# A two-layer hybrid attention and mixture-of-experts step: modulation pieces placed anew, rotary swap by copies, one branch instead of two, the expert count in a bank of its own

## The reference

```
for l in range(2):
    sh1, sc1, gt1, sh2, sc2, gt2 = split(silu(cond) @ w_ada[l] + b_ada[l])   # 1024 x 6144 per layer
    h = rms_norm(y, g_attn[l]) * (1 + sc1) + sh1
    q, k, v of three kinds = h @ w_in[l]            # neighbourhood, latent (MLA), banded window (SWA)
    mla_q, kpe, swa_q, swa_k get a rotary embedding  # sample tokens only
    y = y + gt1 * (merge of the three attentions @ w_out[l])
    h = rms_norm(y, g_ffn[l]) * (1 + sc2) + sh2
    scores = sigmoid(h @ w_router); each token picks 2 of 16 experts of one group
    y = y + gt2 * sum over its experts of (silu(h @ w_gate) * (h @ w_up) * gate) @ w_down
out = rms_norm(y, g_final)                          # and the new caches of keys and values
```

## Time and profile before

| what | value |
|---|---|
| median of 3 runs (lowest, highest) | 1347.58 us (1346.36, 1349.18) |
| the profiled execution's own time | 1345.4 us |
| its span, first to last instruction | 1343.5 us |
| busy time of PE, DVE, ACT, POOL | 1178.3, 777.1, 623.0, 111.8 us |
| mean granted clock of PE | 0.922 |
| scores and values of layer 0, first score to the output projection | 170.99 to 299.65 us |
| the same of layer 1 | 837.78 to 913.41 us |
| experts' products, last of layer 0, last of layer 1 | end 690.99 and 1299.2 us |

### The profile page before, as it was taken

The page is one execution under the profiler, slowest core; times in us unless marked ns, Lnnn a source line. Parts: engine busy times, 40 slices in busy tenths (PEclk is TensorE's granted clock), DMA queues, the critical chain, the costliest instruction groups (busy, mean ns, idle before and its releaser), DMA issues.

```text
span 1343.5 us, 15058 instructions
## 1 busy us (share of the span) xinstructions
PE 1178.3 (88%) x5638; PEld 858.7 (64%) x5638; DVE 777.1 (58%) x1068; ACT 623.0 (46%) x739; POOL 111.8 (8%) x124
## 2 busy tenths in 40 slices
PE   5599887779879999999948998889769999999956
PEld 4266444345467888888836764555467888888846
DVE  1212343341658888988825023572477898888835
ACT  2100233430346777778622003561237777877721
POOL 4000020000010110111001001100010011101000
PEclk8799999999869999999975999899859999999985
DMA  9973377861738999999829233001218999999612
GB/s 261 337 248 117 103 265 250 254 248 63 297 113 317 368 366 372 376 372 378 311 103 276 79 121 94 15 1 58 74 62 303 372 383 369 376 370 369 243 56 97
DMA packets 88702, 310.23 MB, mean 231 GB/s; under 512 B 31272, under 2 KB 35620, under 8 KB 76348
## 3 DMA queue, kind: packets, MB, share of 16 engines
q1 hardware_dynamic: 65548, 279.17, 57.2%
q0 software_dynamic: 11792, 18.65, 4.6%
q10 hardware_dynamic: 11296, 11.54, 2.7%
HBM read 307.07 MB, written 24.27 MB: 247 GB/s over the span
## 4 chain that ended last, share of the span: by engine, by line
PE 78%; DVE 7%; issue 4%; DMA 4%; ACT 4%; ACTq 2%; SPq 1%; POOL 0%; POOLq 0%; DVEq 0%
PE bank L780 15%; PE bank L1011 13%; PE bank L1005 13%; PE bank L1006 13%; DMA ring<-in_w_ada 3%; ACT work L1206 3%; PE bank L762 3%; PE bank L884 2%; PE bank L995 2%; PE bank L787 2%; PE bank L898 2%; PE bank L985 2%; PE bank L707 1%; ACTq L1178 1%; PE bank L831 1%
## 5 line engine op out<-in xcount | busy, mean ns | idle before, releaser
L1680 DVE TENSOR_TENSOR ring_r<-ring,work_r 128x4096 fp32r<-128x4096 f32 x96 | 421.6, 4417 | 5.8 <-ACT work_r L1256 5.6
L1256 ACT ACTIVATE work_r<-ring 128x4096 fp32r<-128x4096 f32 x96 | 348.5, 3632 | 139.7 <-PE bank L1006 120.7
L1005 PE MATMUL bank<-work_r 128*128 128x512 f32 x768 | 311.9, 406 | 21.5 <-ACT work_r L1256 9.6
L1006 PE MATMUL bank<-work_r 128*128 128x512 f32 x768 | 305.0, 397 | 0.0
L780 PE MATMUL bank<-hT,ring 128*128 128x384 f32 (+1 forms) x640 | 213.2, 492 | 5.2 <-ACT hT L1132 3.8
L1011 PE MATMUL bank<-ring_r,work_r 128*128 128x512 f32 x768 | 195.0, 396 | 0.4 <-DVE ring_r L1680 0.4
L1005 PEld LDWEIGHTS bank<-work_r 128*128 128x128 f32 x768 | 148.4, 193 | 53.6 <-issue 19.2
L780 PEld LDWEIGHTS bank<-hT,ring 128*128 128x128 f32 (+1 forms) x640 | 120.8, 191 | 90.3 <-issue 11.4
L1006 PEld LDWEIGHTS bank<-work_r 128*128 128x128 f32 x768 | 148.0, 193 | 29.7
L1011 PEld LDWEIGHTS bank<-ring_r,work_r 128*128 128x128 f32 x768 | 144.2, 188 | 34.7 <-DVE ring_r L1680 0.8
L1104 ACT ACTIVATE work<-bank 128x384 f32<-128x384 f32 (+6 forms) x79 | 37.4, 495 | 198.7 <-PE bank L780 94.1
(11 more groups left out here) (200 smaller groups left out, 1151.3 us busy)
## 6 DMA issues: line engine op xcount, KB each, us to landing
ring<-in_w_gate SPq DMA_DIRECT2D x32, 2048.0 KB, 7.8
ring<-in_w_up SPq DMA_DIRECT2D x32, 2048.0 KB, 10.8
ring<-in_w_down SPq DMA_DIRECT2D x32, 2048.0 KB, 10.4
ring<-in_w_ada SPq DMA_DIRECT2D x24, 2048.0 KB, 8.6
ring<-in_w_in SPq DMA_DIRECT2D x4, 2048.0 KB, 13.5
work<-yscr ACTq DMA_DIRECT2D x12, 512.0 KB, 6.1
ring<-in_w_out SPq DMA_DIRECT2D x4, 1280.0 KB, 8.3
ring<-in_w_in SPq DMA_DIRECT2D x12, 256.0 KB, 8.5
```

Source lines behind the costliest of these rows:

```text
L1005: mm(b[:], x_hi[:, k, :], hi[:, k, half, :], start=(k == 0), stop=False)
L1006: last = mm(b[:], x_lo[:, k, :], hi[:, k, half, :], start=False, stop=False)
L1256: A_(w_hi[:, slot % 2, :], ring[slot][:], ACT.Copy).then_inc(s_hi, 1)
L1680: tt(ring_r[slot][:], ring[slot][:], w_hi[:, slot % 2, :].bitcast(F32), ALU.subtract).then_inc(s_lo, 1)
```

## The change

Six things are changed.

1. Pieces. `ADA_ATT` has 10 pieces instead of 16, one in every second step, with job A before job B. Four pieces of layer 1 (4 to 7) stand between the layers (`BETWEEN`): three A and one B behind the experts, one B behind the first two turned blocks, one B behind the sums, one A behind the spread root and its B between the first two projections. Two pieces (10, 11) stand round the router of layer 1. The router of layer 0 keeps four. The ring order follows, and SP's wait for `s_yl` is moved from the third chunk of layer 1 to its fifth.
2. The SWA swap is done by eight ACT copies per layer between groups of 32 partitions. The four permutation matmuls go, and DVE's nine operations on the three query tiles become three.
3. The count of tokens goes to bank 7, behind the signal that the ranks are done, and DVE reads it after the first expert's tokens are split. The constant `iota` is one higher, so that DVE makes the rank in one operation instead of three.
4. The last list of tokens (`slots(NG - 1)`) is stored behind the first low part of the weights instead of ahead of it.
5. The two branches behind the experts are nested, so that one is passed when no expert has over 128 tokens.
6. The read-back of the experts' rows is three DMAs instead of six.

```diff
-ADA_ATT = [(0, c) for c in range(4, N_ADA)] + [(1, c) for c in range(8)]
-ADA_ROUTE = [(1, c) for c in range(8, N_ADA)]
+ADA_ATT = [(0, c) for c in range(4, 10)] + [(1, c) for c in range(4)]
+ADA_ROUTE = [[(0, 10), (0, 11), (1, 8), (1, 9)], [(1, 10), (1, 11)]]
+ADA_BETWEEN = [(1, c) for c in range(4, 8)]
...
+STREAM[1] = [("ada", *x) for x in ADA_BETWEEN] + STREAM[1] + [("ada", *x) for x in ADA_ROUTE[1]]
...
-    put("iota", i[None, :])
+    put("iota", i[None, :] + 1)
...
+BETWEEN = [f"{kind}{x}{c}" for kind, i in zip("AAABBBAB", (0, 1, 2, 0, 1, 2, 3, 3)) for x, c in [ADA_BETWEEN[i]]]
+BETWEEN_LAST, BETWEEN_ROWS, BETWEEN_SUMS, BETWEEN_SPREAD, BETWEEN_FIRST = (BETWEEN[:4], BETWEEN[4:5], BETWEEN[5:6], BETWEEN[6:7],
+                                                                          BETWEEN[7:])
...
+        def further_passes(eng, most, run, skip, p=1):
+            with eng.If(most > P * p):
+                run(p)
+                if p + 1 < PASSES:
+                    further_passes(eng, most, run, skip, p + 1)
+            with eng.Else():
+                skip(p, PASSES - p)
...
-                    if k == 2:
-                        sp.wait_ge(s_yl[NT - 1], 16 * TOPK * l)
+                    if k == 4:
+                        sp.wait_ge(s_yl[NT - 1], 16 * l)
...
-                read_out(pe, (l, "swk"))
-                b = fill_begin((l, "rk"))
-                filled((l, "rk"), mm(b[:, 0:TS], cv("rot"), swk[:, TP:T], start=True, stop=True))
...
-                read_out(pe, (l, "swq2"))
-                for i in range(3):
-                    b = fill_begin((l, f"rq{i}"))
-                    filled((l, f"rq{i}"), mm(b[:, 0:TS], cv("rot"), swq[:, i, TP:T], start=True, stop=True))
...
+                def swapped_halves(dst, src):
+                    half = HD // 2
+                    for a in range(0, P, half):
+                        to = a ^ half
+                        last = A_(dst[to:to + half], src[a:a + half], ACT.Copy)
+                    return last
+                read_out(act, (l, "swk"))
+                swapped_halves(swk_sw, swk[:, TP:T]).then_inc(s_swapk, 1)
                 for i in range(3):
                     copy((l, f"swq{i}"), swq[:, i, :], T, scale=SCALE)
+                read_out(act, (l, "swq2"))
+                swapped_halves(swq_sw, swq[:, :, TP:T]).then_inc(s_swapq, 1)
...
+                act.wait_ge(s_qkv, l + 1)
                 for i in range(NS + LAG_T):
...
+                    last = mm(b[:, t * NE:(t + 1) * NE], cv("tri"), m[:, t, :], start=(t == 0), stop=True)
+                filled((l, "rank"), last)
                 for t in range(NT):
-                    last = mm(b[:, 3 * NE:4 * NE], ones, m[:, t, :], start=(t == 0), stop=(t == NT - 1))
-                filled((l, "rank"), last)
+                    last = mm(banks[7][:, 0:NE], ones, m[:, t, :], start=(t == 0), stop=(t == NT - 1))
+                last.then_inc(s_counted, 1)
...
+                for j in BETWEEN_LAST if l == 0 else []:
+                    if JOB[1, j][0] == 5:
+                        pe.wait_ge(s_ys, done * NE)
+                    ada(j, 1)
                 pe.wait_ge(s_ys, done * NE)
...
-                    for k in range(TOPK):
-                        act.dma_start(yl[:, t, k, :], yscr[k * T + t * P:k * T + (t + 1) * P, :]).then_inc(s_yl[t], 16)
+                    act.dma_start(yl[:, t], yscr.rearrange("(k t p) d -> t p k d", k=TOPK, p=P)[t]).then_inc(s_yl[t], 16)
+                for j in BETWEEN_LAST + BETWEEN_ROWS if l == 0 else []:
+                    ada_row(1, j)
...
-                chain(nc.vector.tensor_reduce(cnt[:, 0:1], b[:, 3 * NE:4 * NE], AX.X, ALU.max))
-                tc(cnti[:, 0:1], cnt[:, 0:1]).then_inc(s_cnt, 1)
-                evac((l, "rank"), ts(rank, b[:, 0:NT * NE], 1.0, None, ALU.add))
+                evac((l, "rank"), stt(rank, b[:, 0:NT * NE], 1.0, R[4], ALU.add, ALU.mult))
...
-                chain(tt(rank, rank, R[4], ALU.mult))
-                chain(ts(rank, rank, -1.0, None, ALU.add))
...
+                    slots(NG - 1)
                     tokens_rest(0)
+                    if p == 0:
+                        v.wait_ge(s_counted, l + 1)
+                        chain(nc.vector.tensor_reduce(cnt[:, 0:1], banks[7][:, 0:NE], AX.X, ALU.max))
+                        tc(cnti[:, 0:1], cnt[:, 0:1]).then_inc(s_cnt, 1)
+                    v.wait_ge(s_slot, NG * (n + 1))
...
+                for j in BETWEEN_LAST if l == 0 else []:
+                    ada(1, j)
                 add_rows(0)
```

158 lines of the change are left out of this document (88 added, 70 removed).

## The result

The changed kernel takes 1306.85 us (median of 4 runs, 1304.62 to 1314.02) where the kernel before took 1346.97 beside it: ratio 0.9708, 95% interval 0.9686 to 0.973. Run again in a later set it took 1309.60 (1308.92 to 1311.74) against 1347.62, ratio 0.9724 (0.9693 to 0.9754). So 38 to 40 us went, not 29.5. The profiled execution is 1304.66 us, its span 1302.5.

A forecast was written before the change was run, and what follows sets the result against it. PE was taken as the bound, with 78% of the chain. Terms of -19.8 - 5.0 - 1.05 - 0.4 - 3.5 + 1.0 - 0.7 = -29.5 us took 1345.4 to 1315.9, plus 2.2 to the median: 1318 us, range 1309 to 1329.

The forecast's parts named there:

- The 16 pieces explain 53.03 us, 3.31 each: Layer 0's attention: 128.66 us against layer 1's 75.63 without pieces; six pieces fewer at 3.3 gain 19.8 us.
- The second reading: Layer 0's attention: a step with a piece, 6.31 us, less one without, 3.07, prices a piece at 3.24 us.
- The new pattern is the pair that costs 9.38 now: Layer 0's attention: one step with a piece and one without together keep taking 9.38 us.
- Swap: Ahead of the first score: copies replacing swap matmuls gain 2.4 us in layer 0 and 2.6 in layer 1, together 5.0.
- Rank and count in layer 1: Layer 1's routing: DVE loses a 0.62 us wait and most small operations, less one more piece's store; 1.05 us gained.
- Router of layer 0: Rank and count in layer 0: only two of five DVE operations go, as the last piece's jobs remain; 0.4 us gained.
- Last list: Ahead of the experts: DVE's large operation moves before the last list, PE starts 1.75 us earlier per layer; 3.5 gained.
- Between the layers: Layer boundary: queue costs 1.0 us, last A and B 0.5, fewer read-back DMAs gain 0.5; sum 1.0 lost.
- The queue that I feared: Between the layers: first B ahead of turned rows, its store ahead of the first row sum; 1.0 us lost.
- Nested branches: nothing on the path: Behind the experts: engines pass their branches while scatter (3.90 us) or read-back (5.58) runs, so no gain.
- slower than before: Rival on the swap: slow copies between partition groups delay DMA issues in both layers; 1354 us at 6 us each, chance 0.03.
- the warm tail: Rival between the layers: clock stays up through sums of squares, swap and read-back reach their ends; 1311 us, chance 0.08.

The follow-up runs named there:

- e1: Changed kernel with the six moved pieces back (16 in layer 0's attention, two of three steps, B ahead of A, old SP wait): 1332.29 us.
- e9: Changed kernel with the same ten attention pieces in two of three steps, B ahead of A: 66.62 us from step 6 to 21; whole time not given.
- e2: Changed kernel with the rotary swap by permutation matmuls again, for queries and keys: 1307.89 us.
- e8: Changed kernel with the count in the rank's bank again and DVE's further count and rank operations ahead of the lists: 1312.46 us.
- e5: Changed kernel with the further passes as two branches one behind the other again, each skipped by itself: 1313.19 us.
- e15: Changed kernel with flat branches and the four pieces between the layers left out (their values stay zero): 1309.41 us.

## Why the prediction was wrong

The changes of the first profile (41.0 us, of which the start took 0.4 back), with the forecast beside them:

- **Pieces out of the attention: 23.3, forecast 19.8.** The step that failed is "The 16 pieces explain 53.03 us, 3.31 each". It makes one price of several: 128.66 - 75.63 - 10 x 3.73 leaves 15.7 us, 2.6 each, for the six pieces outside steps 6 to 21. The cheap ones are the four in the first six steps: there layer 0 took 27.5 us and layer 1 19.5, 3.25 a step instead of 2.8, with a wait of 3.67 us for DVE among them. So these four cost 2.0 each. What left was the dear kind, 3.7 (e1). The second reading took 3.07 us for a step without a piece, but layer 1's take 42.05 / 15 = 2.80. "The new pattern is the pair that costs 9.38 now" was wrong too: pairs take 7.6 to 10.1 us, by the tile on which the piece falls, and the ten that stayed became cheaper where they met the third tile (3.57 on average, e9 against the changed kernel: 2.8 us of attention).
- **Swap: 4.3 by the first profile, 2.4 to 3.7 by e2, forecast 5.0.** The miss is in layer 1: of PE's 3.52 us I took 2.6, but the value products behind the wait lost their clock, and 1.1 was left.
- **Rank and count in layer 1: 2.26, forecast 1.05.** I set the wait at 0.62 and counted the stores of the moved pieces against it. In the changed kernel's surroundings the wait is 1.27 (e8), and the stores fall before the rank. What the two pieces of that stage, counted as 0.7 gained, did is open: by e8 they cost 0.1 (69.98 - 2.26 = 67.7 against 67.86), by e1, the changed kernel's rank without them, they gave 0.5 (68.38 against 67.86).
- **Router of layer 0: 3.8 in one profile and 0.6 in the other, forecast 0.4.** Clock. Against the average of all fourteen, 72.8, it is 2.0, with only one profile of the kernel before.
- **Last list: 3.45, forecast 3.5.** Right, and by its mechanism.
- **Between the layers: 1.5 gained (tail 1.2, next stage 0.3), forecast 1.0 lost.** B and its store were done before the landing, or together with it. The gain itself is within the spread of the tail (32.6 to 34.3). The queue that I feared is real, but it costs only with the second branch (e5). "Nested branches: nothing on the path" held in layer 0 as long as no pieces stood there, not beside the pieces: I priced two edits apart that work together. In layer 1 it failed too, by 1.0.
- **Not forecast: about 3 us** in small parts (0.5 to 0.9) over the experts of both layers, the tail of layer 1 and its attention. The tail's 0.6 fits the 1.0 that two branches cost there (e5, e15). From the sixth to the last low product layer 0 took 258.4 us before and 257.5 to 258.0 in all others but one, 258.6 with the count as before (e8). So 0.9 may belong to the count; one profile does not show it, and the rest stays open.

The working has a slip that the result did not meet: in the rival "slower than before" the gain to outweigh is 29.5 - 5.0 = 24.5, not 34.5, so the limit is c = 4.3 us, and at 6 us the time is about 1361, not 1354. And the stretch from 708 to 714 us, read there as one of turned rows at a clock of 0.50, holds 1-column sums as well, so it does not tell which of the two leaves the clock low.

Of the rivals only the warm tail lay on the right side, and it is not what happened: the sums of squares still took 6.83 us.

```profile
680.03 6.83 PE L731 MATMUL bank<-cst,hT 128*128 128x1 f32 x32
```

## What to carry to other kernels

A mean over a stage prices the average piece of added work; what leaves or stays is priced by the steps in which it stands, so read the interval step by step, against the same step without it, in a stretch at one clock. Work laid into an engine's wait is free only in full view of what delays its start there: price it together with the branches and waits ahead of it, not edit by edit. And where a small matmul signals together with a larger block, look at who waits for the first part alone.

## What the runs showed of the hardware

- PE passed one skipped branch in 2.2 to 3.3 us of idle time (thirteen profiles) and two in 8.25 (one).
- Flat branches made the tail of layer 1 1.0 us longer than nested ones, with nothing laid into its waits.
- The value products behind a wait of 3 us took 4.54 us at a mean granted clock of 0.62, and 2.93 at 0.94 where other matmuls stood between.
- The same instructions met different clocks in executions of one kernel: A of 1.92 or 3.64 us, a stage of 71.0 or 74.2. Where a single profile is compared with another, differences below 3 us in such a stage say nothing.
- The three A behind an idle 8.25 us took 7.65 us, behind 2.2 to 3.3 us 5.4 to 7.05; in windows (busy us of the engines, then the granted clock) the first 5 us of the former ran at 0.50, and once up the clock stayed so through B and the waits:

```profile
670.00:675.00 5.00, 4.27 (x21) 1.12 (x24) 0.00 (x0) 0.51 (x1) 0.00 (x0) 0.50 1.02 405
675.00:680.00 5.00, 3.96 (x36) 1.24 (x28) 0.96 (x3) 0.68 (x2) 0.00 (x0) 0.96 0.53 213
680.00:685.00 5.00, 2.89 (x25) 2.69 (x26) 4.20 (x13) 1.19 (x3) 0.00 (x0) 1.00 0.86 292
```
